# Attention stage of a hybrid decoder: mask and minimum fused into SBUF, scores ahead of the turning, two banded units first

## The reference, cut to what matters

```
# MLA: 4 heads, query and key of 64 + 32 rotary, values of 64; per 128-query block
sc = einsum('bqhd,bkhd->bhqk', qi, k) * scale
sc = where(kpos <= qpos, sc, -inf)
out = softmax(sc) @ v

# SWA: 4 heads, 2 key heads; per 128-query block the block's keys and those before it
sc = where(0 <= WINDOW + i - j < WINDOW, einsum(q, k) * scale, -inf)    # 128 x 256
pr = softmax(concatenate([sc, sink]))[..., :-1]
out = pr @ v
```

## Time and profile before

| what | value |
|---|---|
| runs | 2324.16, 2321.28, 2320.54 us; median 2321.28 |
| profiled execution, first to last instruction | 2319.9 us |
| busy: PE, PE weight loads, DVE, ACT, POOL | 97%, 80%, 70%, 48%, 44% of the span |
| attention stage, layer 0 | 326.9 to 438.0 us |
| attention stage, layer 1 | 1458.8 to 1567.0 us |

### The profile page before, as it was taken

One profiled execution on the slowest core, in us unless ns is written; L12 is line 12 of the kernel. 1 busy time (PEld: TensorE's weight loads), 2 busy tenths in 40 slices (PEclk: granted clock), 3 DMA queues, 4 the chain that ended last, 5 costly groups with the idle time before them and its releaser, 6 DMA issues.

```text
span 2319.9 us, 31032 instructions
## 1 busy us (share of the span) xinstructions
PE 2259.9 (97%) x11401; PEld 1853.4 (80%) x11401; DVE 1633.3 (70%) x2098; ACT 1102.8 (48%) x1817; POOL 1021.4 (44%) x660
## 2 busy tenths in 40 slices
PE   7999999999999999999999999999999999999998
PEld 6888867887788888888878787778878888888887
DVE  7985468449867666778888744772796767667886
ACT  5355557434444444444543464772454444444455
POOL 3222368445887777300012224053389777760000
PEclk7999999999999999999999999999999999999999
DMA  9742243242333333487466131114323333347763
GB/s 329 283 129 70 63 118 119 110 136 64 103 120 97 116 98 107 161 279 256 146 219 242 54 87 55 37 38 164 119 63 106 114 91 114 91 136 259 256 207 114
DMA packets 271301, 317.13 MB, mean 137 GB/s; under 512 B 33613, under 2 KB 188032, under 8 KB 270383
## 3 DMA queue, kind: packets, MB, share of 16 engines
q1 hardware_dynamic: 269359, 312.11, 41.7%
q10 hardware_dynamic: 1072, 2.23, 0.5%
q0 software_dynamic: 720, 0.81, 0.1%
HBM read 248.37 MB, written 62.54 MB: 134 GB/s over the span
## 4 chain that ended last, share of the span: by engine, by line
PE 84%; DVE 7%; issue 3%; ACT 2%; DMA 1%; SPq 1%; POOL 1%; DVEq 0%; ACTq 0%; POOLq 0%
PE bank L1561 31%; PE bank L1124 19%; PE bank L1576 17%; PE bank L1184 6%; PE bank L1343 1%; PE bank L1424 1%; DVE hLo L2227 1%; PE bank L1452 1%; ACT swaProb L1948 1%; SPq L536 1%; DVE xT L2221 1%; DMA adaw<-in_ada_w_dram 1%; PE bank L1274 1%; DVE xT L2562 1%; DVE tLo L2631 1%
## 5 line engine op out<-in xcount | busy, mean ns | idle before, releaser
L1044 POOL TENSOR_TENSOR wLo<-raw,wHi 128x1024 fp32r<-128x1024 f32 x66 | 161.2, 2443 | 408.6 <-ACT wHi L1046 408.6
L1754 POOL TENSOR_TENSOR prodLo<-comb,prodHi 128x512 fp32r<-128x512 f32 x160 | 233.9, 1468 | 122.4 <-ACT prodHi L1086 122.4
L1561 PE MATMUL bank<-tHi,prodHi 128*128 128x512 f32 x640 | 250.5, 391 | 4.8 <-DVE tLo L2631 4.1
L1561 PE MATMUL bank<-tLo,prodHi 128*128 128x512 f32 x640 | 250.0, 391 | 0.0
L1561 PE MATMUL bank<-tHi,prodLo 128*128 128x512 f32 x640 | 249.8, 390 | 0.0
L1576 PE MATMUL bank<-gateHi,downHi 128*128 128x512 f32 x616 | 240.6, 391 | 0.0
L1576 PE MATMUL bank<-gateHi,downLo 128*128 128x512 f32 x616 | 240.0, 390 | 0.0
L1576 PE MATMUL bank<-gateLo,downHi 128*128 128x512 f32 x616 | 239.9, 390 | 0.0
L1086 ACT ACTIVATE prodHi<-comb 128x512 fp32r<-128x512 f32 x160 | 100.5, 632 | 248.9 <-PE bank L1561 231.2
L2576 DVE SCALAR_TENSOR_TENSOR ub<-bank,ffp,ub 128x1023 f32<-128x1023 f32 x88 | 112.8, 1282 | 141.8 <-ACT ub L2034 140.2
L1561 PE MATMUL bank<-hHi,prodHi 128*128 128x512 f32 x480 | 187.3, 390 | 6.3 <-POOL prodLo L1754 3.7
(11 more groups left out here) (424 smaller groups left out, 5434.9 us busy)
## 6 DMA issues: line engine op xcount, KB each, us to landing
raw<-in_ffn_w_up_dram SPq DMA_DIRECT2D x88, 512.0 KB, 4.7
gateRaw<-gateOut SPq DMA_DIRECT2D x154, 256.0 KB, 4.2
adaE<-in_ada_w_dram SPq DMA_DIRECT2D x64, 512.0 KB, 6.6
gateOut<-gateSums SPq DMA_DIRECT2D x22, 1024.0 KB, 5.5
raw<-in_w_in_dram SPq DMA_DIRECT2D x34, 512.0 KB, 4.1
downRaw<-in_ffn_w_down_dram SPq DMA_DIRECT2D x66, 256.0 KB, 3.6
raw<-in_w_out_dram SPq DMA_DIRECT2D x28, 512.0 KB, 3.8
downCols<-in_ffn_w_down_dram SPq DMA_DIRECT2D x24, 512.0 KB, 3.7
```

The source lines that it names most:

```text
L1044: eng.tensor_tensor(lo[:], raw[slot][:], fview(hi[:]), ALU.subtract).then_inc(s["split_lo"], 1)
L1561: last = mm(o, w[idx][:, c0], moving(idx, kp, hi), start=kp == 0 and q_ == 0, stop=kp == 3 and q_ == 2)
L1754: pool.tensor_tensor(sLoW[idx][:], product_source(js, idx), fview(sHiW[idx][:]), ALU.subtract).then_inc(s["us_lo"], 1)
```

## The change

- `least`: for each head one `tensor_tensor_reduce` reads the scores from PSUM, adds a mask, writes the sums to SBUF and accumulates their minimum. Banded: four operations in place of two, with the sink as the start value. Causal: the mask is `wide`, 768 columns of zeros and then the causal block of 128, from which a slice is taken so that the block falls on the diagonal; blocks of 1024 columns take two operations with a link.
- Masks change sign (`NEG` to `FAR`); POOL makes `wide` ahead of the squares of the scan (`wide_mask`).
- `exps`: causal units too go in place in SBUF. `pr` has four buffers, two of them where the early parts of an output weight lay; these (`out0_hi`, `out0_lo`) move elsewhere, and their making waits for a set of scores.
- `scores(u)` waits for the minimum of u-2 (`un_n`) instead of its exponentials, and PE's order is S(u+2), T(u), V(u-1). DVE's order is the minimum of u+2, then the copy of u.
- Units: the first two banded units lead the stage, then causal units 0 to 6, banded, 7 and so on; from the tenth unit on the order is as before. So S(0) and S(1) wait only for the pieces of mlaV; the waits for query parts and rope DMAs move to S(2) and S(3).
- ACT makes the sinks ahead of the two copies of mlaV. DVE's order ahead of the stage is query parts 0 and 1, the minimum of unit 0, query parts 2 and 3, the minimum of unit 1.

```diff
-BANDED_BEFORE = (4, 6, 7, 9, 11, 17, 19, 21)
+BANDED_BEFORE = (0, 0, 7, 9, 11, 17, 19, 21)
...
+    wide = place("causalWide", [P, T - P], F32, R[15] + 512)
...
-    pr = [place(f"prob{i}", [P, T], F32, at["hl"] + 4 * K * i) for i in range(2)]
+    pr = [place(f"prob{i}", [P, T], F32, a) for i, a in enumerate((at["hl"], at["hl"] + 4 * K, at["f"] + 8 * K, at["f"] + 12 * K))]
...
@@ scores @@
                 if u < 2:
                     pe.wait_ge(s["mp_kv"], nth("mp_kv", 10 + u))
-                    pe.wait_ge(s["mp_q"], nth("mp_q", 10 + 2 * u))
-                    if u == 0:
-                        pe.wait_ge(s["k_rope"], nth("k_rope", 16 * 14))
-                    else:
-                        pe.wait_ge(s["uproj_loaded"], nth("uproj_loaded", 16 * 14))
                 else:
-                    pe.wait_ge(s["un_e"], nth("un_e", u - 1))
+                    pe.wait_ge(s["un_n"], nth("un_n", u - 1))
+                if u == 2:
+                    pe.wait_ge(s["mp_q"], nth("mp_q", 10))
+                    pe.wait_ge(s["k_rope"], nth("k_rope", 16 * 14))
+                if u == 3:
+                    pe.wait_ge(s["mp_q"], nth("mp_q", 12))
+                    pe.wait_ge(s["uproj_loaded"], nth("uproj_loaded", 16 * 14))
...
@@ PE's order @@
             for u in range(NU + 1):
+                if u + 2 < NU:
+                    scores(u + 2)
                 if u < NU:
                     transposes(u)
-                if u + 2 < NU:
-                    scores(u + 2)
...
@@ POOL @@
+            def wide_mask():
+                pool.wait_ge(s["sd_y"], nth("sd_y", NB))
+                pool.wait_ge(s["pack_used"], nth("pack_used", N_WIN))
+                pool.memset(wide[:, 0:T - 2 * P], 0.0).then_inc(s["sd_y"], 1)
+                pool.tensor_copy(wide[:, T - 2 * P:T - P], band[:, 1, :]).then_inc(s["sd_y"], 1)
...
+                    wide_mask()
                     scan_squares()
...
@@ exps, causal @@
-                    if u >= 2:
-                        act.wait_ge(s["un_t"], nth("un_t", u - 1))
                     for q, h in enumerate(hs):
-                        last = A(pr[u % 2][:, q * HALF:q * HALF + n], bank[u % 2][:, q * HALF:q * HALF + n], ACT.Exp,
-                                 bias=st_[:, 0, h:h + 1], scale=-1.0, accum_out=st_[:, 1, h:h + 1])
+                        a = pr[u % 4][:, q * HALF:q * HALF + n]
+                        last = A(a, a, ACT.Exp, bias=st_[:, 0, h:h + 1], scale=-1.0, accum_out=st_[:, 1, h:h + 1])
...
@@ least @@
-                    s4 = bank[u % 2][:].rearrange("p (h k) -> p h k", h=4)[:, :, lo:256]
-                    link(dve.tensor_tensor(prs[i % 2][:, :, lo:256], s4, band[:].rearrange("p b k -> p (b k)")[:, lo:256].unsqueeze(1).to_broadcast([P, 4, 256 - lo]),
-                                           ALU.subtract))
-                    dve.tensor_reduce(st_[:, 0, :], prs[i % 2][:, :, lo:257], AX.X, ALU.min).then_inc(s["un_n"], 1)
+                    for h in range(SWA_H):
+                        last = dve.tensor_tensor_reduce(out=prs[i % 2][:, h, lo:256], in0=bank[u % 2][:, h * 256 + lo:(h + 1) * 256],
+                                                        in1=band[:].rearrange("p b k -> p (b k)")[:, lo:256], scale=1.0, scalar=nsink[:, h:h + 1],
+                                                        op0=ALU.add, op1=ALU.min, accum_out=st_[:, 0, h:h + 1])
                 else:
...
-                    link(dve.tensor_tensor(diag, diag, band[:, 1, :].unsqueeze(1).to_broadcast([P, k, P]), ALU.subtract))
-                    dve.tensor_reduce(st_[:, 0, hs[0]:hs[0] + k], sc[:, :, 0:n], AX.X, ALU.min).then_inc(s["un_n"], 1)
+                    n = (i + 1) * BLK
+                    if u == 2:
+                        dve.wait_ge(s["sd_y"], nth("sd_y", NB + 2))
+                    if u >= 4:
+                        dve.wait_ge(s["un_t"], nth("un_t", u - 3))
+                    for q, h in enumerate(hs):
+                        sc, to = bank[u % 2][:, q * HALF:q * HALF + n], pr[u % 4][:, q * HALF:q * HALF + n]
+                        near, least_of = max(n - (T - P), 0), st_[:, 0, h:h + 1]
+                        if near:
+                            link(dve.tensor_tensor_reduce(out=to[:, 0:near], in0=sc[:, 0:near], in1=wide[:, 0:near], scale=1.0, scalar=FAR,
+                                                          op0=ALU.add, op1=ALU.min, accum_out=least_of))
+                        last = dve.tensor_tensor_reduce(out=to[:, near:n], in0=sc[:, near:n], in1=wide[:, T - P - (n - near):T - P], scale=1.0,
+                                                        scalar=least_of if near else FAR, op0=ALU.add, op1=ALU.min, accum_out=least_of)
+                last.then_inc(s["un_n"], 1)
...
@@ DVE's order @@
-            least(0)
+            for h in range(MLA_H):
+                dve.wait_ge(s["mp_kv"], nth("mp_kv", 6 + h))
+                dve.scalar_tensor_tensor(out=qLo[h][0:64, :], in0=bank[2 + h // 2][64 * (h % 2):64 * (h % 2) + 64, :], scalar=-MLA_SCALE,
+                                         in1=fview(qHi[h][0:64, :]), op0=ALU.mult, op1=ALU.subtract).then_inc(s["mp_q"], 1)
+                if h == 1:
+                    least(0)
             least(1)
             for u in range(NU + 3):
+                if u + 2 < NU:
+                    least(u + 2)
...
                     copy_probs(dve, u, "d", "un_cd")
...
-                if u + 2 < NU:
-                    least(u + 2)
```

More of the change, by code:

```diff
@@ L65 @@
 SWA_SCALE = float(SWA_D ** -0.5)
-NEG = -1.0e30
+FAR = 1.0e30
 N_WIN = 20
@@ L164 @@
 MLA_UNITS = [(i, hs) for i in range(NB) for hs in (((0, 1), (2, 3)) if (i + 1) * BLK <= HALF else ((0,), (1,), (2,), (3,)))]
-BANDED_BEFORE = (4, 6, 7, 9, 11, 17, 19, 21)
+BANDED_BEFORE = (0, 0, 7, 9, 11, 17, 19, 21)
 UNITS = []
 for _n, _unit in enumerate(MLA_UNITS):
-    if _n in BANDED_BEFORE:
-        UNITS.append(("s", BANDED_BEFORE.index(_n), (0, 1, 2, 3)))
+    UNITS += [("s", _i, (0, 1, 2, 3)) for _i in range(NB) if BANDED_BEFORE[_i] == _n]
     UNITS.append(("m",) + _unit)
@@ L266, in build @@
     early_lo = place("earlyLo", [P, 1024], F32R, at["f"] + 8 * K)
+    out0_hi = place("out0Hi", [P, 1024], F32R, at["h"])
+    out0_lo = place("out0Lo", [P, 1024], F32R, at["h"] + 16 * K)
     cs = place("cs", [P, T], F32, at["f"] + 16 * K)
@@ L1032, in _, with home @@
                 sp.wait_ge(s["out_written"], 16 * NB)
+        def home(n, slot):
+            if n == N_OUT0:
+                return out0_hi, out0_lo
+            if n == N_PRE + 2:
+                return early_hi, early_lo
+            return (third_hi, third_lo) if n == 2 else (wHi[slot], wLo[slot])
         def split(eng, slot, n, landed, *slot_free):
@@ L1042, in split @@
             if eng is nc.gpsimd:
-                hi, lo = (early_hi, early_lo) if n in (N_OUT0, N_PRE + 2) else (third_hi, third_lo) if n == 2 else (wHi[slot], wLo[slot])
+                hi, lo = home(n, slot)
                 eng.tensor_tensor(lo[:], raw[slot][:], fview(hi[:]), ALU.subtract).then_inc(s["split_lo"], 1)
             else:
-                eng.activation((early_hi if n in (N_OUT0, N_PRE + 2) else third_hi if n == 2 else wHi[slot])[:], raw[slot][:], ACT.Copy).then_inc(s["split_hi"], 1)
+                eng.activation(home(n, slot)[0][:], raw[slot][:], ACT.Copy).then_inc(s["split_hi"], 1)
         def split_pre(eng, n):
             if n == N_OUT0:
-                split(eng, n % 2, n, loaded(n), ("mp_full", 8))
+                split(eng, n % 2, n, loaded(n), ("un_s", OUT0_HI_AT + 1))
             elif n in (N_OUT0 + 1, N_OUT0 + 2):
@@ L1139, in tile_of @@
             def tile_of(n, w):
[L1140 to L1144, removed]
+                tile = home(n, n % 2)[0 if w is wHi else 1]
+                return lambda k: tile[:, k * P:(k + 1) * P]
             def h_hi(k):
@@ L1423, in transposes @@
                             c0 = slice(q * HALF + b * P, q * HALF + (b + 1) * P)
-                            last = pe.transpose(bank[2][:, c0], pr[u % 2][:, c0], ident[:])
+                            last = pe.transpose(bank[2][:, c0], pr[u % 4][:, c0], ident[:])
                 last.then_inc(s["un_t"], 1)
@@ L1436, in values @@
                     return
+                if u == 0:
+                    pe.wait_ge(s["mp_q"], nth("mp_q", 12))
                 if i and hs[-1] in (1, 3) and (kind == "s" or hs[-1] == 1):
@@ L1928, in _ @@
                 A(qHi[h][0:64, :], rows_of(2, h), ACT.Copy, scale=-MLA_SCALE).then_inc(s["mp_kv"], 1)
-            for u in range(2):
-                act.wait_ge(s["mp_full"], nth("mp_full", 7 + u))
-                A(vt[:, 4 * u:4 * u + 4, :], bank[u][:].rearrange("p (b d) -> p b d", b=4), ACT.Copy).then_inc(s["mp_kv"], 1)
             act.wait_ge(s["sd_yd"], nth("sd_yd", NB))
@@ L1938, in _ @@
                 A(prs[i][:, :, 256], nsink[:], ACT.Copy).then_inc(s["sw_m"], 1)
+            for u in range(2):
+                act.wait_ge(s["mp_full"], nth("mp_full", 7 + u))
```

(5 more changed lines are left out.)

9 lines of the change are left out of this document (3 added, 6 removed), and 2 rows, old and new, of the table PER_LAYER.

## The result

The changed kernel takes 2330.6 us, the median of 7 runs (2326.21 to 2333.61), against 2321.28 before: a ratio of 1.0039 with a 95% interval of 1.003 to 1.0049. It is slower by 9.3 us, where 2320 was forecast. Its profiled execution has a span of 2331.7 us, 11.8 more than that of before; it is one of the longer ones (2333.52 us, 2.9 above the median).

The account below looks back on a forecast made before the run. PE was taken to bound the kernel, busy 97% of the span. Start +7.0, late waits -6.8 and clock -1 summed to -0.8 on a span of 2319.9, written as 2320 us, range 2309 to 2331.

Parts of the forecast that it names:

- the clock: PE's low-clock stretches behind the stage's idle starts: -1 us over both layers, ends -3 and +1.5.
- a low stretch in the stage's middle: Sign of being wrong: PE's low clock coming again in the middle of the attention stage.
- C: Rival: accumulator readout on DVE costs 0.2 us instead of 0.08, late waits stay; +8, 2329 us; chance 0.10.
- The start: PE's waits at the attention stage's start in both layers: 5.3 and 5.2 us against 2.6 and 0.94, together +7.0.
- D: Rival: fused DVE operation takes two cycles a column, so DVE bounds the stage; about +20, 2341 us; chance 0.07.
- The late waits: PE's scattered waits after the stage's starts, 13.3 us over both layers: 6.5 kept, 6.8 gained; bounds 0 and 13.3.
- ACT's copies of probT: Part of PE's waits after the starts, released by ACT's copies: 2.7 us kept of 6.1.
- the waits for banded exponentials: Part of PE's waits after the starts, released by exponentials of banded units: 2.6 us kept of 3.6.
- DVE's copies: Part of PE's waits after the starts, released by DVE's copies behind its minimum: 1.2 us kept of 2.0.
- B: Rival: the scores' lead removes all 13.3 us of scattered waits, low stretch covers idle; -9.3, 2312 us; chance 0.30.
- E: Rival: ACT's queue order sets the waits, no lead, only 1.55 us goes; +5.5, 2327 us; chance 0.13.
- The mask on POOL: Making the wide mask ahead of POOL's squares: about 1 us, ends 0.8 and 2.5, covered by 4 us of slack.

Follow-up runs that it names:

- e10: Kernel before with only mask and minimum fused into SBUF, four prob buffers and exponentials in place; units, PE and DVE orders old: 2316.34 us, ratio 0.9978.
- e3: Changed kernel with DVE's part of the probT copy put back ahead of its minimum: 2324.29 us, ratio 1.0012 to the kernel before.
- e12: Changed kernel with old order of units, all query parts ahead of the first minimum, DVE's copy ahead of its minimum, one-column square sums: 2309.17 us, ratio 0.9946.
- e1: Changed kernel with the 32 square sums of a layer streaming 64 columns each instead of one: 2321.76 us, ratio 1.0005 to the kernel before.
- e11: Changed kernel, new unit order kept, with all query parts first, DVE's copy ahead of its minimum and 64-column square sums: 2313.74 us, ratio 0.9968.

## Why the prediction was wrong

**The step that failed is the clock.** "I take -1 over both layers; ends -3 and +1.5 (one more such stretch, from the longer idle)", says the prediction. It measured +9.6, and not from idle: 10.2 in two long stretches with PE full of small units and sums of one column, 1.7 in the third, less the 1.7 of 1482 and 0.6 at the starts. For the starts alone the term was near (-0.6 against -1). I had counted only what an idle start does to the clock, two stretches of 3.3 us, and passed over the third one in the trace of the kernel before, at 1482 to 1486, in front of which PE was full; and I looked at which units follow the start for their waits alone. The text did name a low stretch in the stage's middle as what would make it wrong. The time stands at the upper edge of the range and outside the forecast's own. C's time, 2329, is the nearest to it by luck: its cause, a dear readout, is out (below).

**The start**: +7.0 expected, +4.2 measured (3.8 and 4.0 us against 2.6 and 0.94). The order of waits was right. The sum was too high, in the main because the fused minimum is shorter than priced, and because turning 1 waited 0.67 us instead of 1.2. At 3.8 and 4.0 us the start's idle is just under the 4 that the prediction had named as a sign of being wrong. DVE's forms over the whole span:

```profile
L2471 DVE CUSTOM_DVE_ANT_0 swaProb<-bank,band,negSink 128x256 f32<-128x256 f32 x56 | 23.6, 477 | 2.7 <-PE bank L1391 2.6
...
L2471 DVE DVE_READ_ACCUMULATOR2_ANT stat_s<- 128x1 f32 x64 | 5.2, 81 | 0.0
```

and its timeline (one operation, its readout, the next):

```profile
332.00 0.48 DVE L2471 CUSTOM_DVE_ANT_0 swaProb<-bank,band,negSink 128x256 f32<-128x256 f32 x1
332.41 0.08 DVE L2471 DVE_READ_ACCUMULATOR2_ANT stat_s<- 128x1 f32 x1
332.41 0.48 DVE L2471 CUSTOM_DVE_ANT_0 swaProb<-bank,band,negSink 128x256 f32<-128x256 f32 x1
```

The next operation starts with the readout: 0.41 us apart, not 0.51. Four take 1.63, where 2.04 was forecast, and the wait for the minimum of unit 1 was 1.8, not 2.45. With that cases C (a readout of 0.15 and more) and D (two cycles a column) are out: 256 columns in 0.41. DVE became 13 us lighter a layer, not 7 to 9. The Trainium skill, "VectorE: DVE Perf Modes", section "Two Vector instructions with no wait between them", counts an operation with an accumulator as two instructions, and the trace shows two; the second costs no time of its own here. The Trainium skill, "VectorE: DVE Perf Modes", section "Rules for kernel authors", would not have one fuse for speed; e10 measures 0.22% gained by fusing with what comes with it, and the measurement decides.

**The late waits**: 6.8 gained of 13.3 expected, 5.2 measured (8.1 left: idle 15.8 less 7.7 at the starts). That the sum is near is luck, for its parts were not. ACT's copies of probT were kept at 2.7 and measured 0; the waits for banded exponentials at 2.6, measured 0.7 (3.9 less 3.2 at the starts). DVE's copies were kept at 1.2 and measured 7.0: I named that DVE takes the minimum ahead of the copy and priced it for banded units only. e3 shows that putting the copy first costs 0.4 us a layer elsewhere. B is out with the 8.1 us that stayed, and E with the waits for ACT's copies that went: the lead of the scores was real, and e12 against e10 shows its worth, 7 us.

**The mask on POOL**: about 1 us expected and hidden, so measured:

```profile
307.03 0.74 POOL L1703 MEMSET causalWide<- 128x768 f32 x1
307.71 0.29 POOL L1704 COPY causalWide<-band 128x128 f32<-128x128 f32 x1
```

By the measured terms the sum is +4.2 - 5.2 + 9.6 = +8.6, against 11.8 between the two profiled executions, from which the terms are read, and 9.3 between the medians.

## What to carry to other kernels

Give the clock a term of its own when an order changes: list what PE streams, before and after, and not only where it waits, and look through the trace of before for low stretches that no idle explains; work placed by unit number lands beside other work when the units are reordered. Where a change brings several things, price and time them apart: here fusing and scores in front were worth 10 us, the new order, with its split query parts, cost 10 by itself and 19 on top of them. And where a producer is put ahead of a copy on one engine, compare the copy's consumer with the longest producer of the whole stage, not of the unit in view.

## What the runs showed of the hardware

- PE's granted clock fell to 1.2 GHz with PE busy 4.00 and 3.91 of 4.00 us in the two windows before the one of the fall (changed kernel, layer 0), behind 16 matmuls of one streamed column. With 64 columns in place of one it stayed at 2.4 GHz there (e1, e11).
- Sixteen matmuls with 128 columns of weights took 1.84 and 1.92 us with one streamed column (changed kernel, first groups of the layers) and 1.89 to 1.97 with 64 (e1), at the higher clock: the wider ones were all but free.
- The fused add and minimum on DVE, one input in PSUM and one in SBUF, written to SBUF, came every 0.41 us for 256 columns, its accumulator's readout of 0.08 beside the start of the next one; one of 896 columns took 1.08 (mean of eight, with a constant as the start value).
